# A gated DeltaNet inside a two-block network: the squared lengths of the keys are summed by ScalarE over the token-major copy instead of by TensorE

## What is computed

```python
def _l2norm(x):
    xf = x.astype(jnp.float32)
    return xf * lax.rsqrt(jnp.sum(jnp.square(xf), axis=-1, keepdims=True) + RMS_EPS)

def project(h):
    p = h @ w_in
    qkv = jax.nn.silu(_centred_dwconv(p[..., :n_qkv], conv_w))     # 5 taps along the tokens
    q = _l2norm(qkv[..., :hk].reshape(bsz, L, 8, 128)) * (128 ** -0.5)
    k = _l2norm(qkv[..., hk:2 * hk].reshape(bsz, L, 8, 128))
    v = qkv[..., 2 * hk:].reshape(bsz, L, 8, 128).astype(f32)
    ...
# then, for both directions, a chunked delta rule over blocks of 64 tokens, with q, k, v and gates
```

## Time and profile before

| | us |
|---|---|
| median of 3 runs | 4196.18 |
| lowest, highest | 4194.09, 4201.79 |
| the profiled execution | 4192.13 |
| its span in the trace | 4190.3 |

### The profile page before, as it was taken

How to read it: one execution, slowest core, us unless ns; L and a number is a source line. 1 busy time by engine, 2 the same in 40 slices (tenths; PEclk the granted TensorE clock), 3 DMA queues, 4 the chain that set the end, 5 groups by cost and what they waited for, 6 DMA issues and landing times.

```text
span 4190.3 us, 67649 instructions
## 1 busy us (share of the span) xinstructions
PE 3888.3 (93%) x28266; PEld 3189.0 (76%) x28266; DVE 2149.4 (51%) x3078; ACT 1665.1 (40%) x2708; POOL 617.2 (15%) x676
## 2 busy tenths in 40 slices
PE   6999999788999988987899899999999998899999
PEld 4887777677888866756788675778888878778887
DVE  3667754753222453377323654555665428655564
ACT  3444444422112242263323346554334335544333
POOL 0044555522000001003000000000210003000120
PEclk8999999898999999999999899999999999999999
DMA  5244443321121121103222320221323230312332
GB/s 162 89 154 133 146 147 127 131 89 61 61 71 51 60 88 52 49 1 112 81 95 91 71 81 11 74 100 62 100 94 105 89 111 3 130 65 81 101 101 81
DMA packets 235991, 367.67 MB, mean 88 GB/s; under 512 B 9811, under 2 KB 142630, under 8 KB 235302
## 3 DMA queue, kind: packets, MB, share of 16 engines
q1 hardware_dynamic: 217200, 300.49, 21.8%
q0 software_dynamic: 17936, 62.70, 4.9%
q10 hardware_dynamic: 550, 0.17, 0.0%
HBM read 344.36 MB, written 18.96 MB: 87 GB/s over the span
## 4 chain that ended last, share of the span: by engine, by line
PE 76%; DVE 14%; ACT 7%; issue 2%; DMA 1%; POOL 0%; ACTq 0%; DVEq 0%; SPq 0%; POOLq 0%
PE psum L259 21%; PE psum L260 20%; PE psum L261 20%; PE psum L256 13%; DVE arena L289 4%; ACT arena L389 3%; PE psum L265 2%; DVE arena L299 2%; DVE rw L289 2%; DVE rx L383 2%; DVE arena L303 1%; ACT arena L393 1%; ACT rw L393 1%; DVE arena L315 1%; ACT rx L393 1%
## 5 line engine op out<-in xcount | busy, mean ns | idle before, releaser
L259 PE MATMUL psum<-rx,rw 128*128 128x512 f32 (+2 forms) x2864 | 1057.8, 369 | 51.6 <-DVE rx L383 27.9
L260 PE MATMUL psum<-rx,rw 128*128 128x512 f32 (+2 forms) x2864 | 1031.8, 360 | 0.0
L261 PE MATMUL psum<-rx,rw 128*128 128x512 f32 (+2 forms) x2864 | 1030.0, 360 | 0.0
L289 DVE TENSOR_TENSOR rw<-arena,rw 128x2048 fp32r<-128x2048 f32 (+3 forms) x266 | 545.5, 2051 | 811.8 <-ACT rw L393 802.1
L256 PE MATMUL psum<-arena 32*32 32x32 f32 (+8 forms) x12982 | 769.4, 248 | 116.5 <-ACT arena L393 44.3
L256 PEld LDWEIGHTS psum<-arena 32*32 32x32 f32 (+4 forms) x12982 | 583.1, 133 | 263.9 <-issue 89.3
L393 ACT ACTIVATE rw<-arena 128x2048 fp32r<-128x2048 f32 (+3 forms) x266 | 453.6, 1705 | 755.8 <-PE psum L261 739.8
L259 PE MATMUL psum<-rw,rx 128*128 128x512 f32 (+1 forms) x1720 | 681.4, 396 | 31.0 <-DVE rx L383 13.9
L259 PEld LDWEIGHTS psum<-rx,rw 128*128 128x128 f32 (+1 forms) x2864 | 550.9, 192 | 183.9 <-DVE rx L383 41.4
L260 PE MATMUL psum<-rw,rx 128*128 128x512 f32 (+1 forms) x1720 | 672.7, 391 | 0.0
L261 PE MATMUL psum<-rw,rx 128*128 128x512 f32 (+1 forms) x1720 | 672.3, 391 | 0.0
(11 more groups left out here) (73 smaller groups left out, 2206.9 us busy)
## 6 DMA issues: line engine op xcount, KB each, us to landing
arena<-in_ffn_w_up SPq DMA_DIRECT2D x66, 1024.0 KB, 5.0
arena<-in_ada_w SPq DMA_DIRECT2D x48, 1024.0 KB, 5.9
arena<-in_ffn_w_down SPq DMA_DIRECT2D x40, 1024.0 KB, 4.9
arena<-in_ffn_w_gate SPq DMA_DIRECT2D x22, 1024.0 KB, 5.1
arena<-in_dn_w_in SPq DMA_DIRECT2D x16, 1024.0 KB, 5.9
arena<-in_xa_w_kv SPq DMA_DIRECT2D x16, 1024.0 KB, 4.9
arena<-in_hgrn_w_in SPq DMA_DIRECT2D x16, 1024.0 KB, 5.5
arena<-in_da_w_in SPq DMA_DIRECT2D x12, 1024.0 KB, 5.0
```

Source lines behind the costliest of these rows:

```text
L259: self.e.matmul(out, l[0], r[0], start=start, stop=False)
L260: self.e.matmul(out, l[0], r[1], start=False, stop=False)
L261: return self.e.matmul(out, l[1], r[0], start=False, stop=stop)
L289: return self.e.tensor_tensor(out, a, b, op)
```

## The change

For keys, the sums move from TensorE to ScalarE. ScalarE no longer squares the channel-major copy, and TensorE no longer does the six matmuls. Instead `act_part_tok`, after its own copy `tok_a`, waits for VectorE's copy `tok_d` and runs six Square instructions of 128 columns with an accumulated output, one for each group of tokens, into the array of sums. The 1e-6 of a key part is added by VectorE two parts later, in the post step of the query part. Queries are as before. The waits on `dn_ss` go for keys; the slot of the token-major copy is overwritten only after the squares of the key part before it have been made.

```diff
@@ pe_part_post
-    if part in (K_, Q_):
+    if part == Q_:
         p.wait_ge(*K.at("dn_sq", r))
         b = p.bank("ss", r, among=among)
@@ act_part_tok
         a.free("dn_tok", r, 0)
+    if STREAM[r][2] == K_:
+        a.wait_ge(*K.at("tok_d", r))
+        if r >= DENSE:
+            a.wait_ge(*K.at("G_st", 0))
+        for c in range(6):
+            a.act(K.mem(CO + 2016, 128), tok_mem(K, r)[:, c, :], ACT.Square, accum_out=part_sums(K, r)[:, c:c + 1]).then_inc(
+                *a.sig(("k_sq", r)))
+
+
+def part_sums(K, r):
+    hg, h4, part = STREAM[r]
+    return norm_mem(K, hg)[0].rearrange("p (q c h) -> p q c h", q=2, c=6)[:, 1 - part, :, h4]
@@ dve_conv
-                if STREAM[before][2] != V_:
+                if STREAM[before][2] == Q_:
                     v.wait_ge(*K.at("dn_ss", before))
@@ dve_part_post
-    if part in (K_, Q_):
-        ss = norm_mem(K, hg)[0].rearrange("p (q c h) -> p q c h", q=2, c=6)[:, 1 - part, :, h4]
+    if part == Q_:
+        ss, sk = part_sums(K, r), part_sums(K, r - 2)
+        v.wait_ge(*K.at("k_sq", r - 2))
+        v.ts(sk, sk, 1e-6, None, ADD).then_inc(*v.sig())
         v.wait_ge(*K.at("dn_ss", r))
         v.ts(ss, K.ps("ss", r)[:, 0:6], 1e-6, None, ADD).then_inc(*v.sig(*[("ss_eps", hg)] if r == LAST_Q[hg] else []))
         v.free("ss", r)
     if part in (K_, V_):
         v.wait_ge(*K.at("dn_tok", r))
         tok_free(v, K, r)
+        if tok_before(r) is not None and STREAM[tok_before(r)][2] == K_:
+            v.wait_ge(*K.at("k_sq", tok_before(r)))
         v.cp(tok_mem(K, r)[:, 4:6, :], r2(K.ps("dn_tok", r, 1)[:, 0:256], 2)).then_inc(*v.sig(("tok_d", r)))
```

## The result

The changed kernel takes 4214.95 us (median of five runs, 4210.12 to 4220.46), the kernel before 4194.46 us beside it (five runs, 4190.19 to 4201.79): ratio 1.0047, 95% interval 1.0037 to 1.0058, so 0.47% slower; the medians lie 20.5 us apart. The traced execution spans 4216.3 us against 4190.3 us. The forecast said slower, 4208 us, with a range of 4197 to 4218: direction and range hold; the size entered was +11.5 us, and 20.5 us came.

The account below looks back on a forecast made before the run. The prediction took the dense stage to be bound by VectorE's and ScalarE's loop, within about a microsecond of TensorE. Queues +6.4, clock +5.1 and rounds about 0 made +11.5 us: 4196.2 to 4207.7, say 4208 us, range 4197 to 4218.

Parts of the forecast that it names:

- The loop of VectorE and ScalarE: Dense stage: convolution and Silu loop takes 19.4 us for two parts, as TensorE does; whatever is added shows in the end.
- The walk through the queues: Dense stage, iteration by iteration: the delay of each convolution's start, leaving the stage 6.4 us later by the queues alone.
- Six squares 2.6 us, table load 1.28 us exposed in iteration 3: ScalarE, dense stage: squares ahead of the next Silu take 2.6 us; iteration 3's formerly hidden table load adds 1.28 us.
- The rival with cheap squares: Squares run 0.2 us apart, so three iterations lose 1.4 us less each; total 4202 us, chance 0.06.
- TensorE waits 6 to 8 us, and 5 us: Dense stage: TensorE idles 6 to 8 us before the Square of part 2 and 5 us before part 6's.
- The clock: After each of two dense-stage waits TensorE runs 5 us at half clock, 2.5 us lost each; +5.1 us passes on.
- the 9 us of the third row: Trace before the change: half clock lasted 9 us after a 2.13 us wait; used for both waits, about +9 us.
- The rival with the clock up: Queues cost 6.4 us, but TensorE's clock stays up or slow stretches fall into waits; 4202.6 us, chance 0.16.
- Dense stage +11.5: Sum for the dense stage: 6.4 us from the queues and 5.1 us from TensorE's clock.
- The rounds about 0: Rounds: TensorE's 1.25 us saved at each of four posts cancels against ScalarE's 2.6 us; bounds -2.5 to +6.
- the main case (4203 to 4212): Whole kernel: queues and clock delay the dense stage, the rounds add about 0; chance 0.57.
- the fourth rival: Rounds lose too: ScalarE's late pieces reach TensorE at parts 16 and 17, or slow stretches last 9 us; 4213, chance 0.15.

Follow-up runs that it names:

- experiment 4: The changed kernel, filled with matmuls of 128x512 that nobody reads ahead of TensorE's two long waits: 4201.31 us, ratio 1.0015 to the kernel before.
- experiments 2 and 6: Against the changed kernel: ScalarE copies all six key blocks, 4189.44 us; squares issued later, 4192.12; first order in dense stage with second in rounds, 4188.56.
- the second trace: The changed kernel, with no edit, traced once more: 4214.68 us.
- the second pair of traces: The kernel before and the changed kernel, neither edited, each traced once more: 4193.0 and 4214.68 us.

## Why the prediction was right, and where its sizes were off

- **The loop of VectorE and ScalarE sets the end of the dense stage, not TensorE's 93%.** Right. 6.4 to 7.8 us more in the loop turned 7.3 us less TensorE work into a loss (experiment 4), and only taking the squares out of the loop let TensorE's gain show (experiments 2 and 6).
- **The walk through the queues.** Right to half a microsecond up to conv(9). Foreseen conv(3) at 122.5 (+3.6), conv(5) +3.0, conv(6) +5.2, conv(7) +6.9, conv(9) +6.4; the filled kernel, where the clock takes no part, has +3.7, +3.2, +5.5, +7.3 and +6.9, and the changed one has conv(3) at 121.63 + 0.9 = 122.5. In the filled kernel the term ended at +7.8 where 6.4 was entered: there the value parts do not just carry the difference on. (The changed kernel has its 14.6 us already at conv(9).)
- **Six squares 2.6 us, table load 1.28 us exposed in iteration 3.** 2.58 us (114.60 to 117.18) and 1.28 us (117.19 to 118.47). Against the Trainium skill ("ScalarE: Activation LUTs", What ACT_TABLE_LOAD costs): no 1.38 us of drain stands between the accumulator's read, the load and the Silu at 118.48, and the estimate of 1.2 us for the six, from that section's figures for the plain form, is under half of what they took. The rival with cheap squares falls by the same rows.
- **TensorE waits 6 to 8 us, and 5 us.** Right, the first at the upper edge: 8.44 and 5.18, in the second trace 7.46 and 5.17.
- **The clock.** The mechanism was right, the step "I take 5 us" was mis-sized. The slow stretches lasted 8.1 and 8.4 us after work came back (7.5 and 8.1 in the second trace, 5.6 and 7.1 with only the dense stage changed), not 5. Changed less filled is 14.6 - 7.8 = 6.8 us, where +5.1 was entered; half of the slow time is 8.3, 7.8 and 6.3 us. For the changed kernel the 9 us of the third row was the better model, and the reason given against it (that it didn't come before dense work) was no reason. The rival with the clock up is refuted by the windows.
- **Dense stage +11.5.** 14.6 and 14.2, and 12.8 with the rounds left alone. By the filled kernel 1.4 us were too little for the queues and 1.7 for the clock. Taking half of the slow time off each of the three instead leaves 6.3, 6.4 and 6.4 us, just what was entered for the queues, and then the clock's term alone was too small. The runs don't decide between the two, for the filled kernel also has 52 matmuls more.
- **The rounds about 0.** Right up to 500 us. The rounds alone gave +0.3 there. In the changed kernel it was 4.2 in the first trace, over the 4 us named as the mark, but 3.4 of them are the clock, and 1.6 in the second. Posts of 1.25 us less and squares of 2.6 us more cancelled, as walked: 0.97 us of waiting at part 13, none for ScalarE at parts 16 and 17. Their 6.0 us in the medians come behind 500 us and belong to the next point.
- **The missing term.** The sum ended at the rounds. Behind 500 us the second pair of traces differs by 9.2 + 1.6 - 3.8 = 7.0 us, beside a clock's sum of 10.2 us. With dense +13.6 and this +7.0 the 20.5 us are there. The sum had no place for it: it took for granted that a lag, once made, passes through unchanged. It comes mostly with the rounds' parts: behind 205 us the trace with the dense stage's four alone adds 1.0 us, the one with the rounds' four alone 7.1. Nothing in the forecast accounts for these 7 us: they lift the result above the main case (4203 to 4212), and it lies in the range only by the 6 us kept for a loss in the rounds, which this is not. That this room sufficed is luck. The result lay near the price of the fourth rival (4213). Of its two conditions ScalarE did not reach TensorE at parts 16 and 17, while slow stretches near 9 us (8.1 and 8.4) did come, in the dense stage; they explain 1.7 to 3.2 of the 9.0 us by which the sum was short.

## What to carry to other kernels

When work moves to an engine with idle time, look at what ends that idle time: the squares of four key parts on an engine that is 40% busy cost this stage 14 us where their input came from behind the same convolution as the next step's, and it gained 5 us once they could run before it. Price a new wait of TensorE with the clock behind it, by the longest slow stretch that the trace has and not by the mildest. And check the waits' order first: moving the squares by a few lines was worth more than the whole change.

## What the runs showed of the hardware that was not expected

- Waits of 8.44 and 5.18 us of TensorE were followed by 8.1 and 8.4 us at 1.2 GHz, so the longer wait had no more slow work behind it. The same instructions in another kernel, after 7.75 and 5.19 us, were followed by 5.6 and 7.1 us. With the time filled by matmuls that nobody reads, 1.00 was granted from 110 to 170 us, and the stage ended 6.8 us earlier.
- The same wait of 2.56 us around 785 us was followed by a stretch with mean clock 0.84 in one kernel and 0.50 in another, 11 us each, and each kernel repeated its own in the second trace (0.84 and 0.51). Stages that a change doesn't touch gained or lost 5 us and more: between 500 and 900 us the kernels here differ from the one before by -7.3 to +12.6 us in a stretch, and the clock's sum by -5.1 to +10.2.
